# First two units of each stage taken chunk by chunk with both halves of the weights; convolution of the last feed-forward net read from PSUM

## What is computed

```python
for l in range(2):
    x = x + 0.5*gate * swiglu(adaln_in(x, ...), w1, w3, w2)      # feed-forward 0 and 2
    h = adaln_in(x, ...) @ w_in[l]                               # win0, win1
    x = x + gate * (mixer(h) @ w_out[l])                         # wout0, wout1
    x = x + 0.5*gate * swiglu(adaln_in(x, ...), w1, w3, w2)      # feed-forward 1 and 3
# the third layer
proj = rms_norm(x, attn_norm) @ w_in_2                           # win2
x = x + mixed @ w_out_2                                          # wout2
x = x + memory_cross_attention(...)                              # wmk, wmv, wmq, wmo
gu = rms_norm(x, ffn_norm) @ w_up                                # feed-forward 4
gu = depthwise_conv(gu, ffn_conv_w, ffn_conv_b, 1, 1)            # 3 taps along the tokens
g, u = gu[..., :D_FF_2], gu[..., D_FF_2:]
x = x + (silu(g) * u) @ w_down
```

## Time and profile before

| what | value |
| --- | --- |
| median of 3 runs | 1583.8 us (1580.27 to 1584.36) |
| profiled execution, its own time | 1583.53 us |
| its span, first to last instruction | 1581.6 us |
| TensorE busy | 1468.4 us (93%), 10992 matmuls |
| DVE busy | 1167.4 us (74%) |
| ACT busy | 694.9 us (44%) |
| POOL busy | 87.6 us (6%) |
| mean granted TensorE clock | 0.964 of full speed |
| mean HBM traffic | 194 GB/s over the span |

### The profile page before, as it was taken

How to read it: one execution, slowest core, us unless ns; L and a number is a source line. 1 busy time by engine, 2 the same in 40 slices (tenths; PEclk the granted TensorE clock), 3 DMA queues, 4 the chain that set the end, 5 groups by cost and what they waited for, 6 DMA issues and landing times.

```text
span 1581.6 us, 26637 instructions
## 1 busy us (share of the span) xinstructions
PE 1468.4 (93%) x10992; PEld 1367.2 (86%) x10992; DVE 1167.4 (74%) x1873; ACT 694.9 (44%) x1104; POOL 87.6 (6%) x38
## 2 busy tenths in 40 slices
PE   1999999999999989999899999999989779799998
PEld 1999998788999989998897789999856558699998
DVE  6888987867778788777667666565682656589998
ACT  2433444444434343344445344444535645544443
POOL 0000000000000000010000000000000110033343
PEclk8899999999999999999999999999999879999999
DMA  9986864165777546856332244654402203335442
GB/s 390 413 330 263 334 257 168 49 247 212 300 285 289 215 185 282 338 208 253 132 122 107 107 169 181 237 209 152 160 1 94 107 14 133 121 121 200 179 182 81
DMA packets 32327, 309.29 MB, mean 196 GB/s; under 512 B 3496, under 2 KB 5800, under 8 KB 7504
## 3 DMA queue, kind: packets, MB, share of 16 engines
q1 hardware_dynamic: 32208, 307.60, 50.5%
HBM read 306.53 MB, written 1.06 MB: 194 GB/s over the span
## 4 chain that ended last, share of the span: by engine, by line
PE 83%; DVE 11%; ACT 3%; issue 2%; DMA 1%; SPq 0%; DVEq 0%; ACTq 0%
PE bank L763 13%; PE bank L635 12%; PE bank L631 12%; PE bank L632 12%; PE bank L681 6%; PE bank L683 6%; PE bank L686 6%; PE bank L648 2%; PE bank L601 2%; DVE WL L1635 2%; DVE tmp L1653 1%; PE bank L829 1%; PE bank L840 1%; PE bank L852 1%; DMA X<-in_x 1%
## 5 line engine op out<-in xcount | busy, mean ns | idle before, releaser
L1635 DVE TENSOR_TENSOR WL<-ring,WH 128x1024 fp32r<-128x1024 f32 x398 | 477.4, 1221 | 57.3 <-ACT WH L1141 55.0
L1141 ACT ACTIVATE WH<-ring 128x1024 fp32r<-128x1024 f32 x420 | 429.8, 1053 | 137.1 <-PE bank L763 51.8
L631 PE MATMUL bank<-XH,WH 128*128 128x256 f32 x1680 | 410.1, 283 | 1.4 <-ACT WH L1141 1.4
L632 PE MATMUL bank<-XL,WH 128*128 128x256 f32 x1680 | 407.7, 281 | 0.0
L631 PEld LDWEIGHTS bank<-XH,WH 128*128 128x128 f32 x1680 | 316.2, 188 | 7.6 <-issue 6.0
L632 PEld LDWEIGHTS bank<-XL,WH 128*128 128x128 f32 x1680 | 316.2, 188 | 1.0 <-issue 1.0
L635 PE MATMUL bank<-XH,WL 128*128 128x256 f32 x1680 | 234.4, 282 | 2.9 <-DVE WL L1635 2.9
L635 PEld LDWEIGHTS bank<-XH,WL 128*128 128x128 f32 x1680 | 214.3, 189 | 3.3 <-DVE WL L1635 3.3
L681 PE MATMUL bank<-GH,WH 128*128 128x256 f32 x840 | 203.6, 280 | 1.6 <-DVE GL L1760 1.6
L1214 ACT ACTIVATE SG<-bank 128x256 f32<-128x256 f32 x88 | 33.9, 385 | 387.3 <-PE bank L635 363.6
L683 PE MATMUL bank<-GL,WH 128*128 128x256 f32 x840 | 203.4, 280 | 0.0
(11 more groups left out here) (308 smaller groups left out, 1769.1 us busy)
## 6 DMA issues: line engine op xcount, KB each, us to landing
ring<-in_stream SPq DMA_DIRECT2D x133, 1536.0 KB, 6.6
scr<-in_stream SPq DMA_DIRECT2D x15, 1536.0 KB, 11.0
PR<-in_stream SPq DMA_DIRECT2D x15, 1536.0 KB, 8.3
att<-in_stream SPq DMA_DIRECT2D x15, 1536.0 KB, 10.1
ring<-in_stream SPq DMA_DIRECT2D x8, 1024.0 KB, 4.9
ring<-in_stream SPq DMA_DIRECT2D x11, 512.0 KB, 3.6
kf_mix<-in_stream SPq DMA_DIRECT2D x2, 1536.0 KB, 16.7
con<-in_consts SPq DMA_DIRECT2D x1, 2000.0 KB, 15.4
```

Of the source, the lines that this page charges most:

```text
L631: pe.matmul(o, part(WH, u, k), XH[:, k, :], start=(k == 0), stop=False)
L632: pe.matmul(o, part(WH, u, k), XL[:, k, :], start=False, stop=False)
L1141: act.activation(part_all(WH, u), raw(u), ACT.Copy).then_inc(*mark("high", u))
L1635: dve.tensor_tensor(part_all(WL, u), raw(u), part_all(WH, u).bitcast(F32), ALU.subtract)\
```

## The change

1. `first_up` and `proj_first` go chunk by chunk. For each chunk of the norm: hh and lh of the first unit, hh and lh of the second. Both units' low halves must be there before the second and the fourth matmul. The hl passes still come last. This holds for the five feed-forward nets, for `win0`, `win1`, `win2`, `wmq` and `wmo` and for the second half of `wout2`; `wout0` and `wout1` keep their two groups.
2. The low halves of both first units are split ahead of the norm: `split_to(... + 2)` at the end of a net, and in front of net 0 between the modulation and the scaling.
3. In net 4, ACT computes the middle tap with the bias out of PSUM into `guc` (one ACTIVATE per half), DVE adds the two outer taps out of PSUM (four SCALAR_TENSOR_TENSOR, one link between), and the bank is given back after the last tap (`up_conv`) instead of after the copy (`up_padded`). `gu` and its zeroing are gone.
4. The low half of net 4's `w2` units is made by DVE, too; POOL has no splits left.

```diff
 def low_engine(u):
-    name = UNITS[u][0]
-    return "pool" if name[0] == "w2" and name[1] == 4 else "dve"
+    return "dve"
...
                 def first_up(b):
                     units = list(enumerate(up_units(f, 0)))
-                    for a, u in units:
-                        o = b[:, a * S:(a + 1) * S]
-                        for which, w in ((WH, ("high", u)), (WL, low_of(u))):
-                            pe.wait_ge(*at(*w))
-                            for k in range(KD):
-                                if which is WH and a == 0:
-                                    pe.wait_ge(*at("norm_high", key, k))
-                                pe.matmul(o, part(which, u, k), XH[:, k, :], start=(which is WH and a == 0 and k == 0),
-                                          stop=False, skip_group_check=True)
+                    for k in range(KD):
+                        pe.wait_ge(*at("norm_high", key, k))
+                        for a, u in units:
+                            for which, w in ((WH, ("high", u)), (WL, low_of(u))):
+                                if k == 0:
+                                    pe.wait_ge(*at(*w))
+                                pe.matmul(b[:, a * S:(a + 1) * S], part(which, u, k), XH[:, k, :],
+                                          start=(which is WH and a == 0 and k == 0), stop=False, skip_group_check=True)
...
-            def proj_first(name, passes, groups=(None,)):
+            by_chunk = tuple((k,) for k in range(KD))
+
+            def proj_first(name, passes, groups=by_chunk):
...
             proj("wout2", ...
-                 between=norm_follows("memx"), groups=((0, 1, 2, 3), (4, 5, 6, 7)))
+                 between=norm_follows("memx"), groups=((0, 1, 2, 3),) + by_chunk[4:])
...
                     if f == 4:
-                        act.activation(gu[:, c % 2, :, 1:1 + S], bank[4 + c % 2].rearrange("p (a t) -> p a t", a=2), ACT.Copy)\
-                            .then_inc(*mark("up_padded", c))
+                        for a in range(2):
+                            col = a * NFF + c
+                            last = act.activation(guc[:, c % 2, a, :], bank[4 + c % 2][:, a * S:(a + 1) * S], ACT.Identity,
+                                                  bias=prm("fconv_b", col), scale=prm("fconv_w", 2 * NFF + col))
+                        last.then_inc(*mark("up_tap", c))
...
-                        for a in range(2):
-                            col = a * NFF + c
-                            conv(guc[:, c % 2, a, :], gu[:, c % 2, a, :], 0, 3, lambda k: prm("fconv_w", 2 * NFF * k + col),
-                                 prm("fconv_b", col), last=("up_conv_g" if a == 0 else "up_conv", c))
+                        for k in (0, 2):
+                            for a in range(2):
+                                col = a * NFF + c
+                                o, src = guc[:, c % 2, a, :], b[:, a * S:(a + 1) * S]
+                                o, src = (o[:, 1:S], src[:, 0:S - 1]) if k == 0 else (o[:, 0:S - 1], src[:, 1:S])
+                                ins = dve.scalar_tensor_tensor(o, src, prm("fconv_w", 2 * NFF * k + col), o, ALU.mult, ALU.add)
...
-                split_to(UNIT_AT["w2", f, NFF - 1] + 1)
+                split_to(UNIT_AT["w2", f, NFF - 1] + 2)
...
                 if l == 0:
-                    norm_parts_of(("sub", 0, 0), lambda: split_to(up_units(0, 0)[1]))
+                    split_to(up_units(0, 0)[1])
+                    norm_parts_of(("sub", 0, 0))
```

More of the change, by code:

```diff
@@ L480, in build @@
     net = scr[:, 2496:2496 + 3 * S].rearrange("p (a t) -> p a t", t=S)
-    gu = scr[:, 0:2 * 2 * (S + 2)].rearrange("p (r a t) -> p r a t", r=2, a=2)
     guc = scr[:, 2048:2048 + 4 * S].rearrange("p (r a t) -> p r a t", r=2, a=2)
@@ L623, in up @@
                     b = bank[4 + c % 2]
-                    take(4 + c % 2, *(("g32", f, c) if f < 4 else ("up_padded", c)))
+                    take(4 + c % 2, *(("g32", f, c) if f < 4 else ("up_conv", c)))
                     if c == 0:
@@ L765, in passes @@
                     return last
-                order = order or list(range(kc))
+                order = list(order or range(kc))
                 return passes
-            def proj_first(name, passes, groups=(None,)):
+            by_chunk = tuple((k,) for k in range(KD))
+            def proj_first(name, passes, groups=by_chunk):
                 for ks in groups:
@@ L778, in unit, with proj @@
                 passes(j, ["hh", "hl", "lh"]).then_inc(*mark("product", name, j))
-            def proj(name, high, low, between=lambda j: None, groups=(None,)):
+            def proj(name, high, low, between=lambda j: None, groups=by_chunk):
                 passes = projection(name, high, low, [k for g in groups for k in g or ()])
@@ L864, in win0_and_attention @@
             def win0_and_attention():
-                passes = projection("win0", *norm_parts(("sub", 0, 1)))
+                passes = projection("win0", *norm_parts(("sub", 0, 1)), range(KD))
                 proj_first("win0", passes)
@@ L911, in win1_and_attention @@
             def win1_and_attention():
-                passes = projection("win1", *norm_parts(("sub", 1, 1)))
+                passes = projection("win1", *norm_parts(("sub", 1, 1)), range(KD))
                 proj_first("win1", passes)
@@ L1068, in win2_and_attention @@
                 norm_sum("mem")
-                passes = projection("win2", *norm_parts("attn2"))
+                passes = projection("win2", *norm_parts("attn2"), range(KD))
                 proj_first("win2", passes)
@@ L1123, in _ @@
             attention("e", lambda h: [("act_copied", "wmq", h), ("head_normed", "memk", h), ("mv_copied", 1)])
-            proj("wmo", lambda k: ("mixed", "e", k), lambda k: ("low_att", "e", k))
+            proj("wmo", lambda k: ("mixed", "e", k), lambda k: ("low_att", "e", k), groups=by_chunk[:4])
             norm("ffn2")
@@ L1734, in ffn @@
                 split_to(up_units(f, 0)[1])
[L1735 to L1737 removed]
                 for c in range(NFF):
                     if f == 4:
[L1740 to L1746 removed]
+                        dve.wait_ge(*at("up_tap", c))
+                        b = bank[4 + c % 2]
+                        for k in (0, 2):
[4 more added lines that the diff above has]
+                                ins = dve.scalar_tensor_tensor(o, src, prm("fconv_w", 2 * NFF * k + col), o, ALU.mult, ALU.add)
+                                if k == 2:
+                                    ins.then_inc(*mark("up_conv_g" if a == 0 else "up_conv", c))
+                            if k == 0:
+                                link(ins)
                         split_to(up_units(f, c)[0] + PARTS)
```

12 lines of the change are left out of this document (2 added, 10 removed).

## The result

The changed kernel takes 1564.0 us (median of 4 runs, 1562.9 to 1568.3) against 1583.3 us: ratio 0.9882, interval 0.9867 to 0.9897. The forecast was 1563.0, range 1556 to 1572. The profiled execution is the slowest of the four, 1568.3 us with a span of 1566.5; so its trace is one of a run 4 us over the median, and of the quicker runs there is none.

What follows compares the result with a forecast made beforehand. TensorE, 83% of the chain, was taken as the bound, full inside the nets, leaving mainly the stage starts to win. 12.9 + 3.4 + 0.4 + 2.6 + 1.2 = 20.5 us off 1583.5 gave 1563 us, range 1556 to 1572.

Steps and rivals of the forecast that it cites:

- Part 1, the six stages, 12.9 us: First 48 matmuls of win0, win1, nets 1 to 4: 7.4 us each by chunk, clock back after 3.9 us; gain 12.9.
- Case (a): Six stage starts: clock comes back no earlier, gain 5.5 us for 12.9, kernel at 1570.5 us; chance 15%.
- case (c): Six stage starts: clock doesn't fall at all, gain 20 us for 12.9, kernel at 1556 us; chance 7%.
- The prediction's own sign of being wrong: Stage starts: the low clock after the start lasts 6 us or more.
- rival (b): Mixers behind win0, win1, win2: they absorb the earlier starts, wmq's gain also lost, kernel at 1571 us; chance 12%.
- `win2`, `wmq`, `wmo`, `wout2`, 3.4 us: Mixer stages: thin first pass won, 1.2 us in win2, 1.7 in wmq, 0.5 in wmo, 0 in wout2.
- Net 0, 0.4 us: Net 0's start: both splits push the first matmul to 41.7, units end at 49.1 or 49.7; gain 0.4 us.
- Part 3, 3.8 us: Net 4: gain 2.6 us near its start, 1.2 at its end, nothing in the steady part; product at 0.42 us.
- Part 2, cover: After a net: second split, 1.22 us, fits DVE's 2.32 us idle time ahead of the reciprocal; 0 gain or loss.
- rival (d): Stage starts: second unit's low half is late, dense run waits, 13.6 us for 9.6; kernel at 1600 us; chance 2%.
- The sum: Whole kernel: 12.9 + 3.4 + 0.4 + 2.6 + 1.2 = 20.5 us gain, from 1583.5 to 1563 us.

## Why the prediction was right, point by point

- **Part 1, the six stages, 12.9 us.** The mean of six executions is 7.4 us a stage, as predicted, a gain of 12.9; the profiled one alone has 11.1, its repetition 13.8. The size was right and the mechanism was right in the mean only: the clock doesn't come back 3.9 us behind the start of dense work but at one of several moments, so that a stage takes 6.5, 7.2 or 8.4 us. Case (a) (8.7 a stage) and case (c) (6.2) were given as rivals, and each happens in some stages; that they cancel in the mean is luck. The prediction's own sign of being wrong, a low clock of 6 us or more, stands in two stages of the profiled execution (`win0` and net 3, 2 x 0.36 x 8.5 = 6.1 us). That the low clock is the larger loss, 1.9 us a stage to the thin pass's 1.1, and that it comes from TensorE's idle time, the 24 unread matmuls show.
- **What becomes of it.** Net 1 to net 2 gave its 2.5 us in full, and so did `win0`'s stretch: it gave 1.1 and 1.3 us for the 2.2 forecast because the clock left its 48 matmuls no more (1.1 and 1.3 us shorter), and the mixer behind took nothing. Behind `win1` the 48 are 3.6 and 3.0 us shorter and the stretch 2.7 and 1.5, so that this mixer was 0.9 and 1.5 us longer; in four other runs with the same text up to there it was 0.9 longer, 0.2 shorter and twice 1.6 shorter. Of rival (b) the traces of the change show no more than that ahead of net 3.
- **`win2`, `wmq`, `wmo`, `wout2`, 3.4 us.** This is the step that failed, in `win2`. Its first 48 took 6.1 us for 7.64, as forecast, but from its first matmul to `wout2` it is 171.4 us (174.1 in the repetition) for 170.8. The forecast had let 1.2 us pass the wait for a transfer; that wait became longer instead, 5.6 us for 3.6:

```profile
1130.91 1.06 ACT L1140 ACTIVATE WH<-ring 128x1024 fp32r<-128x1024 f32 x1 [5.62 <-DMA ring<-in_stream]
```

  It ended 8.8 us earlier than before the change, when `win2` had started 9.3 earlier. The wait is one of three terms that the forecast took as fixed and that are not; the others are the clock in the mixer and the clock behind `wout2`. The windows from the end of `win2`'s 48 to `wout2` and from `wout2` to `wmq`, before, changed and repeated:

```profile
1131.91:1295.09 163.18, 135.60 (x706) 97.20 (x705) 91.87 (x160) 85.50 (x176) 11.92 (x10) 0.88 0.19 71
1295.09:1329.96 34.87, 32.96 (x229) 29.81 (x229) 23.02 (x34) 14.35 (x27) 0.00 (x0) 1.00 0.30 106
1121.03:1286.30 165.27, 135.59 (x707) 97.19 (x705) 92.25 (x160) 85.55 (x176) 11.93 (x10) 0.89 0.19 71
1286.30:1322.67 36.37, 34.34 (x228) 31.32 (x229) 23.01 (x34) 14.35 (x27) 0.00 (x0) 0.95 0.29 102
1118.40:1286.46 168.06, 139.43 (x706) 100.51 (x705) 92.30 (x160) 85.55 (x177) 11.92 (x10) 0.86 0.18 69
1286.46:1321.32 34.86, 32.84 (x228) 29.84 (x229) 23.01 (x34) 14.32 (x27) 0.00 (x0) 1.00 0.30 106
```

  The changed kernel lost 2.1 us with the wait, and 1.5 behind `wout2`, where the clock is 0.95 for 1.00. Its repetition lost nothing there but 4.9 us in the mixer, with the wait at 5.35 us and the clock at 0.86. In the run with the old convolution, the same text up to net 4, the wait is 3.59 and the mixer 163.4 us: there net 3 to `wmq` takes 400.9 us, 3.6 less than before the change, as forecast. Over the five executions of this text the stretch is 405.7, 405.5, 405.3, 404.1 and 400.9 us. What makes the wait 3.6 to 3.8 us in some and 5.2 to 5.6 in others is open. `wmq` and `wmo` gave 2.0 for 2.2 in both executions, but 0.3 in two of the others (49.3 us for 47.6, at a clock of 0.93 for 1.00).
- **Net 0, 0.4 us.** The first matmul came at 40.59, not 41.7, the units ended at 48.75 (49.1 and 49.7 were the two readings), and `win0` starts 1.1 us earlier.
- **Part 3, 3.8 us.** Alone it gave 3.8 by the trace (202.1 to 198.3) and 4.8 by the medians. In the changed kernel `down(0)` ends 9.3 us behind the first units (9.6 predicted, 12.3 before), and the last `down` begins 4.9 us behind the last `up` for 5.7: 2.9 and 0.8 for 2.6 and 1.2. The end has less because the product waits 0.5 us for the gate's tap and the activation. The reason given for the long product, POOL beside it, held. The prediction priced the two edits as one; apart they are worth about 1 us each, and the convolution without the move off POOL leaves DVE held about as long as before (2.4 us for 2.6), in another instruction.
- **Part 2, cover.** Right: DVE's idle time of 2.32 us took the split. That it is a condition and not a detail, rival (d) run as an experiment shows, with 13.4 us in `win0` and 14.4 in `win1` for 13.6 worked out.
- **The sum.** 20.5 predicted, 19.3 measured, with 16.3 to 21.1 by the interval. By the two traces the gain is 15.1 and 16.3 us of span, less than by the medians, since both profiled executions were the slowest of their kernel. The one large error in them is 4.4 to 4.6 us from net 3 to `wmq`; every other stretch of the table is within 1.5 us of its forecast in both. Of a quicker one there is no trace. The run with the old convolution shows what one may hold: a span of 1561.9 us, with 13.9 us won in the six stages and 3.6 from net 3 to `wmq`. The terms move by some us from execution to execution, so that the sum came out within 1.2 us is in part luck.

**A faster version.** The changed kernel with 24 or 12 unread matmuls has ratios of 0.9853 and 0.9860 to the kernel before, the changed kernel 0.9882 and 0.9879. All four intervals overlap, so 3 us more are likely and not proved.

## What to carry to other kernels

Where an engine idles ahead of a stage and then works thinly, count the two losses apart: the gaps of the first pass (1.1 us here) and the lower clock behind the idle time (up to 1.9). An order that consumes each input chunk fully as it comes removes the first and shortens the second, but it needs every other operand of the chunk at the start, and the helper work that makes them has to move into a real idle spell first: either half alone gave nothing or a loss here. Follow a gain to the start of the next stage before adding it, and in more than one execution: dense nets passed it on in full, but the mixers' own lengths moved by 1 to 5 us between executions of the same text, as much as a stage had won.

## What was not expected of the hardware

- The clock's return behind an equal idle spell of 3.5 us and equal dense work differs from execution to execution of one program: 6.5, 7.0 to 7.3 or 8.2 to 8.5 us for the same 48 matmuls.
- A thin pass (0.385 us a matmul) begun at full clock, 0.55 us after dense work, still lost the clock in three of six stages.
- A DVE instruction beside a POOL subtraction over two SBUF tiles ended only 0.14 us behind it: a 0.30 us rounding with one input took 2.37.
- The same program text took 400.9 to 405.7 us from net 3 to `wmq` in five executions, and 47.6 or 49.3 from `wmq` to net 4, the longer one at a granted clock of 0.93 for 1.00. Why is open.
